# Turning three sample tiles apart instead of two doubled ones, in the RWKV-7 stage of a hybrid decoder step

## The chip, the cores and the metric

One Trainium2 chip, one NeuronCore. The metric is the device time of one execution in microseconds. A NeuronCore has TensorE (PE: its weight loads are shown apart, as PEld), VectorE (DVE), ScalarE (ACT), GpSimd (POOL), SyncE (SP), which issues DMAs, and 16 DMA engines. Each engine runs its own instructions in order and waits on semaphores for the others. TensorE's clock has two levels here, 1.2 and 2.4 GHz; the profile gives the granted clock as a share of the upper one, so 0.5 is the lower.

## The reference, cut to what matters

One inference step of a two-layer trunk in f32: D = 1024, 512 prompt tokens, and 8 sample sequences of 8 new tokens each. Layer 0 mixes with RWKV-7, layer 1 with a convolution module, and each is followed by an expert retrieval (PEER). The change is in the RWKV-7 mixer, which for each of 16 heads of size 64 keeps a 64x64 state S:

```
def step(S, inp):
    r_t, w_t, k_t, v_t, kk_t, a_t = inp
    sa = jnp.einsum('bhij,bhj->bhi', S, -kk_t)
    S = (S * w_t[:, :, None, :] + sa[..., None] * (kk_t * a_t)[:, :, None, :]
         + v_t[..., None] * k_t[:, :, None, :])
    return S, jnp.einsum('bhij,bhj->bhi', S, r_t)
```

The kernel does not step through the tokens. For a block of tokens it gathers the `sa` rows in a matrix U by solving a triangular system, and then gets the new state as a sum of two outer products over the block's tokens, U with b = kk*a, and V with k. The samples start from their own states (8 sequences), the prompt from zero.

## The kernel before, in words

Everything is feature major: 128 features in the partitions, 576 tokens (512 of the prompt, then 64 of the samples) along the free dimension. The stages follow one another: rmsnorm and low-rank inputs, then `wkv`, then the output projection, then one long stage for both retrievals and the convolution, which goes from about 1002 us to the end of the span. The change touches `wkv` alone. It runs from about 81 to 936 us.

`wkv` is a loop of 8 passes, written by hand for each engine, and a pass does one chunk of 128 features, that is two heads (e = 0, 1; 64 partitions each). The order on each engine is the order of the source; semaphores with named steps (class `Steps`) tie the engines. `X.value("name", i)` is the wait for step "name" of pass i. A pass of PE is:

1. small expansions and the three projections w, k, a, r, norm, v, g, bonus (each projection 32 matmul records of 288 columns),
2. turns of v, b, k into token-major tiles, the Gram matrices of four prompt blocks (L494), and six levels of a triangular inverse (L506, L513, L518),
3. the chain over the four prompt blocks: `rows_R` (L528, L531), `rows_U` (L538), `rows_Y_S` (L543 to L551), each of them waiting for a small copy of ACT or a state update of DVE; the samples' work lies between them,
4. the tail: `s_Y`, "mean" (L621, through `expand` in L449), `s_S` (L625), "var" (the `expand` of `ysq` behind it), after which the next pass begins with "w" (L449) and "k" (L443).

For the samples, three tiles of 128 features by 64 tokens have to be turned so that tokens stand in the partitions: b, k and v. Before, POOL copies the sample columns of all four factors at, rt, bt, kt side by side (`s_factors`, L846), and v's sample columns twice (`s_vv`, L849). PE turns two 128x128 tiles (L577, `s_tok`): b and k together, so that b's tokens are in partitions 0 to 63 and k's in 64 to 127, and v doubled, so that its tokens are in both halves. ACT copies the result into `stok` (L682). The sample state update `s_S` (L625) then takes b and k as one stationary operand over all 128 partitions, and `uv_exp` as moving operand: U expanded by sequence in partitions 0 to 63 (L817), V in 64 to 127 (L814). One matmul for each half of the sequences (h = 0, 1; 512 columns) sums both outer products. DVE takes the result at L825, and updates the state at L827 and L829.

In the trace an f32 matmul shows as two records with a weight load each, and a transpose as one.

Of the kernel before, what the change touches and what calls it, by code (L numbers as in the profile page):

```python
# [16 lines left out]
ALU = mybir.AluOpType  # L17
ACT = mybir.ActivationFunctionType
AX = mybir.AxisListType

P = 128
D = 1024
C = D // P
T = 512
SB, ST = 8, 8
NS = SB * ST
N = T + NS
# [8 lines left out]
LEVELS = 7  # L36
# [72 lines left out]
def unsq(view, axis, n):  # L109

    return view.unsqueeze(axis).to_broadcast(list(view.shape[:axis]) + [n] + list(view.shape[axis:]))
# [183 lines left out]
def wkv(nc, K, I, xm, y_out, hid_wa, hid_g, R, wo_loaded):  # L295
# [8 lines left out]
    f = lambda: R.cut(N)  # L304
# [3 lines left out]
    av, v_s, g_s, nrm = f(), f(), f(), f()  # L308
    e_pos, e_neg = f(), f()
    prev_at = R.at  # L310
    e_prev, factors, bon = f(), R.cut(4, N), f()
    at, rt, bt, kt = (factors[:, j, :] for j in range(4))
    s_factors, s_vv = R.cut(4, NS), R.cut(2, NS)

    ba, rk = lprev, sq
    y_s, yc, ysq, sd = e_pos, e_neg, e_prev, nrm
# [13 lines left out]
    co = [[Q0.cut(NB, P) for _ in range(2)] for _ in range(2)]  # L330
# [9 lines left out]
    Q = Region(K.arena, R.at)  # L340
    s_state = Q.cut(SB, P)
    Q2 = Region(K.arena, l_at)
    stok = Q2.cut(2, P)
    sL, sLT, sX, sXT, sG, sRB, sRK, sco, scoT = (Q2.cut(2, NS, parts=NS) for _ in range(9))
    sy1, sy2 = Q2.cut(2, NS, parts=NS), Q2.cut(2, NS, parts=NS)
    sr_tok, su_tok = Q2.cut(P, parts=NS), Q2.cut(P, parts=NS)
    assert Q2.at <= x_end
    Q3 = Region(K.arena, g_at)
    uv_exp = Q3.cut(SB, P)
    s_prod = Q3.cut(SB, P)  # L350

    wl = [K.sem(f"wkv_w{j}") for j in range(3)]
# [11 lines left out]
    act_s = Steps(K.sem("wkv_act"),  # L364
                  ["w", "k", "ksq", "a", "r", "norm", "exps", "v", "g", "tok_v", "tok_b", "tok_k", "gram_L0", "gram_L1"]
                  + [f"{x}{l}_{e}" for l in range(1, LEVELS) for x in ("y", "X") for e in range(2)]
                  + ["R0", "s_tok", "U0", "s_y1", "R1", "U1", "s_y2", "R2", "U2", "R3", "U3", "s_U"]
                  + ["Y", "ysq", "sd"], a_pass_ahead=True)
    dve_s = Steps(K.sem("wkv_dve"),
                  ["logs", "rk", "factors", "bonus"]  # L370
                  + [f"{x}{e}" for e in range(2) for x in ("maskLT", "level0_", "gramG", "gramRB", "gramRK")]
                  + [f"XT{l}_{e}" for l in range(1, LEVELS) for e in range(2)]
                  + ["s_gram", "state0", "s_X1", "state1", "s_X2", "state2", "s_RT", "state3"]
                  + ["s_y", "s_exp", "yc", "s_state", "y"], a_pass_ahead=True)
    pool_s = Steps(K.sem("wkv_pool"), ["s_copies"] + [f"co{l}_{e}" for l in range(1, LEVELS) for e in range(2)])
    assert NB == 4 and SLEVELS == 3
    ps = K.ps
    lev = lambda l, t: K.level[:, 2 * l + t, :]

    def later(view, l):  # L380

        return view.rearrange("p (g two r) -> p g two r", two=2, r=2 ** l)[:, :, 1, :]

    def packed(view, l):

        return view.rearrange("p (g r) -> p g r", r=2 ** l)

    with nc.Block() as block:
# [48 lines left out]
        def _(pe):  # L437
# [14 lines left out]
            with pe.Fori(0, C) as i:  # L452
# [19 lines left out]
                for src, bank, name, other, ready in ((v_s, 2, "tok_v", act_s, "v"), (bt, 0, "tok_b", dve_s, "factors"),  # L472
                                                      (kt, 1, "tok_k", act_s, "r")):
                    pe.wait_ge(other.sem, other.value(ready, i))
                    for b in range(NB):
                        last = pe.transpose(ps[:, bank, b * P:(b + 1) * P], src[:, b * P:(b + 1) * P], K.ident)
# [4 lines left out]
                for e in range(2):  # L481
                    q = slice(64 * e, 64 * e + 64)
                    for name, left, right, free in (("L", at, bt, ("g", "tok_k")), ("LT", bt, at, ("g", "tok_v")),
# [8 lines left out]
                        for b in range(NB):  # L492
                            t = slice(b * P, (b + 1) * P)
                            last = pe.matmul(ps[:, bank[e, name], t], left[q, t], right[q, t], start=True, stop=True)  # L494
# [3 lines left out]
                for l in range(1, LEVELS):  # L498
                    for e in range(2):
# [5 lines left out]
                        for b in range(NB):  # L505
                            last = pe.matmul(packed(ps[:, 4 * e, b * P // 2:(b + 1) * P // 2], l), co[l % 2][e][:, b, :],  # L506
                                             later(XT[:, e, b, :], l), start=True, stop=True)
                        last.then_inc(pe_s.at(f"y{l}_{e}"), 1)
                    for e in range(2):
                        if (l, e) == (1, 0):  # L510
                            pe.wait_ge(act_s.sem, act_s.value("gram_L1", i))
                        for b in range(NB):
                            last = pe.transpose(ps[:, 4 * e + 1, b * P:(b + 1) * P], XT[:, e, b, :], K.ident)  # L513
                        last.then_inc(pe_s.at(f"turn{l}_{e}"), 1)
                    for e in range(2):
                        pe.wait_ge(act_s.sem, act_s.value(f"X{l}_{e}", i))
                        for b in range(NB):
                            last = pe.matmul(ps[:, 4 * e + 2, b * P // 2:(b + 1) * P // 2], X[:, e, b, :], y1[e][:, b, :],  # L518
                                             start=True, stop=True)
# [4 lines left out]
                def rows_R(b):  # L524
                    t = slice(b * P, (b + 1) * P)
                    if b:
                        pe.wait_ge(dve_s.sem, dve_s.value(f"state{b - 1}", i))
                    pe.matmul(ps[:, 0, 0:P], at[:, t], sc_state[b % 2], start=True, stop=False)  # L528
                    for e in range(2):
                        q = slice(64 * e, 64 * e + 64)  # L530
                        last = pe.matmul(ps[:, 0, q], G[:, e, b, :], ptok[:, 2, b, q], start=False, stop=e == 1)  # L531
                    last.then_inc(pe_s.at(f"R{b}"), 1)
# [40 lines left out]

                pe.wait_ge(dve_s.sem, dve_s.value(f"XT{LEVELS - 1}_1", i))
                rows_R(0)
                for j, src in enumerate((s_factors[:, 2:4], s_vv)):
                    last = pe.transpose(ps[:, 4, j * P:(j + 1) * P], src.rearrange("p a b -> p (a b)"), K.ident)  # L577
                last.then_inc(pe_s.at("s_tok"), 1)
                for e in range(2):
                    q = slice(64 * e, 64 * e + 64)  # L580
                    for j, (left, right) in enumerate(((at, bt), (bt, at), (kt, at), (bt, rt), (kt, rt))):
                        last = pe.matmul(ps[0:NS, 5 + e, j * NS:(j + 1) * NS], left[q, T:N], right[q, T:N],
                                         start=True, stop=True)
# [10 lines left out]
                pe.wait_ge(state_loaded, i * 32 + 32)  # L594
                pe.wait_ge(dve_s.sem, dve_s.value("s_X2", i))
                for h in range(2):
                    pe.matmul(ps[:, 5 + h, :], s_factors[:, 0:2].rearrange("p a b -> p (a b)"), s_state[:, 4 * h:4 * h + 4, :], start=True, stop=True)
                for e in range(2):
                    q = slice(64 * e, 64 * e + 64)
                    last = pe.matmul(ps[0:NS, 4, q], sG[:, e, :], stok[0:NS, 1, q], start=True, stop=True)  # L600
                last.then_inc(pe_s.at("s_RT"), 1)
                rows_R(3)
                rows_U(3)
# [2 lines left out]
                for e in range(2):  # L606
                    q = slice(64 * e, 64 * e + 64)
                    last = pe.matmul(ps[0:NS, 7, q], sXT[:, e, :], sr_tok[:, q], start=True, stop=True)
# [5 lines left out]
                for e in range(2):  # L614
                    q = slice(64 * e, 64 * e + 64)
                    pe.matmul(ps[q, 4, 0:NS], su_tok[:, q], sRB[:, e, :], start=False, stop=False)
                    last = pe.matmul(ps[q, 4, 0:NS], stok[0:NS, 1, q], sRK[:, e, :], start=False, stop=True)
                last.then_inc(pe_s.at("s_Y"), 1)
                pe.wait_ge(dve_s.sem, dve_s.value("s_y", i))
                pe.wait_ge(act_s.sem, act_s.value("Y", i))  # L620
# [1 line left out]
                pe.wait_ge(dve_s.sem, dve_s.value("s_exp", i))  # L622
                for h in range(2):
                    hb = slice(4 * h, 4 * h + 4)
                    last = pe.matmul(ps[:, 6 + h, :], stok[:, 0, :], uv_exp[:, hb, :], start=True, stop=True)  # L625
                last.then_inc(pe_s.at("s_S"), 1)
                pe.wait_ge(act_s.sem, act_s.value("ysq", i))
                expand(K.headones, ysq, 0, "var")
# [2 lines left out]
        def _(act):  # L631
            act_s.begin(act)
            with act.Fori(0, C) as i:
# [45 lines left out]

                rows_R(0)  # L680
                act.wait_ge(pe_s.sem, pe_s.value("s_tok", i))
                act.activation(stok, ps[:, 4, 0:2 * P].rearrange("p (j f) -> p j f", f=P), ACT.Copy).then_inc(act_s.at("s_tok"), 1)  # L682
                rows_U(0)
                for b in (1, 2):
                    act.wait_ge(pe_s.sem, pe_s.value(f"s_y{b}", i))
                    last = act.activation(sy1, ps[0:NS, 7, 0:2 * NS].rearrange("p (e f) -> p e f", f=NS), ACT.Copy)
                    if b < SLEVELS - 1:
                        last = act.activation(sy2, ps[0:NS, 7, 2 * NS:4 * NS].rearrange("p (e f) -> p e f", f=NS), ACT.Copy)
# [15 lines left out]
        def _(dve):  # L704
            dve_s.begin(dve)
            tt, ts, stt = dve.tensor_tensor, dve.tensor_scalar, dve.scalar_tensor_tensor
            dve.memset(s_state, 0.0).then_inc(zeroed, 1)
            with dve.Fori(0, C) as i:
# [102 lines left out]
                dve.drain()  # L811
                tt(sr_tok, s_rows[0:NS, :], ps[0:NS, 4, 0:P], ALU.add).then_inc(dve_s.at("s_RT"), 1)
                update_state(3)
                tt(uv_exp[NS:P], unsq(stok[NS:P, 1, :], 1, SB), unsq(K.seq_of[NS:P], 2, P), ALU.mult)  # L814
                dve.wait_ge(pe_s.sem, pe_s.value("s_Y", i))
                dve.tensor_copy(y_s[:, T:N], ps[:, 4, 0:NS]).then_inc(dve_s.at("s_y"), 1)
                tt(uv_exp[0:NS], unsq(su_tok, 1, SB), unsq(K.seq_of[0:NS], 2, P), ALU.mult).then_inc(dve_s.at("s_exp"), 1)  # L817

                dve.wait_ge(pe_s.sem, pe_s.value("mean", i))
                stt(out=halves(yc), in0=of_banks(ps, 0), scalar=-1.0 / HD, in1=halves(y_s),  # L820
# [2 lines left out]
                for h in range(2):  # L823
                    hb = slice(4 * h, 4 * h + 4)
# [16 lines left out]
        @block.gpsimd  # L841
        def _(pool):
            with pool.Fori(0, C) as i:
                pool.wait_ge(dve_s.sem, dve_s.value("factors", i))
                pool.nop(nofuse=True)
                pool.tensor_copy(s_factors, factors[:, :, T:N])  # L846
                pool.wait_ge(act_s.sem, act_s.value("v", i))
                pool.nop(nofuse=True)
                pool.tensor_copy(s_vv, unsq(v_s[:, T:N], 1, 2)).then_inc(pool_s.at("s_copies"), 1)  # L849
                for l in range(1, LEVELS):  # L850
                    for e in range(2):
                        if l == 1:
                            pool.wait_ge(act_s.sem, act_s.value(f"gram_L{e}", i))
                        if l > 2:
                            pool.wait_ge(pe_s.sem, pe_s.value(f"y{l - 2}_{e}", i))
                        pool.tensor_tensor(co[l % 2][e], L[:, e], unsq(lev(l, 0), 1, NB), ALU.mult).then_inc(pool_s.at(f"co{l}_{e}"), 1)  # L856
# [989 lines left out]
```

## Time and profile before

| | |
|---|---|
| median of 3 runs | 4191.81 us (4189.78 to 4196.97) |
| the profiled execution | 4196.97 us, span 4195.2 us |
| mean granted TensorE clock | 0.939 |
| PE busy, of the span | 3525.0 us (84%), 12440 matmul records |
| DVE busy | 2866.3 us (68%) |
| ACT busy | 1480.4 us (35%) |
| POOL busy | 1482.4 us (35%) |
| in the stretch 81 to 927 us: PE, DVE, ACT, POOL busy | 775.5, 398.0, 255.1, 127.8 us; clock 0.92 |

A profile line names the source line (L625), the engine, the operation, the tensors as out<-in, the shape, and the count. "Idle before" is what the engine waited, with the instruction that ended the wait. Lines of the waits view read: who waited, for whom, total us, times, longest. In a timeline a row may be several instructions of one line merged: start, length, engine, line, shape, count. A stationary shape such as 64*128 is 64 partitions contracted by 128 columns; the moving shape follows. Matmul ends are modelled, so their starts are the better guide.

### The profile page before, as it was taken

What the parts mean: (1) busy time and instruction counts of PE and PEld (TensorE: products, weight loads), DVE (VectorE), ACT (ScalarE), POOL (GpSimd) and SP (SyncE); (2) the same over time, 40 slices, a digit from 0 to 9 for tenths busy, and PEclk for the clock granted to TensorE, in tenths of its full rate; (3) what the DMA queues carried; (4) which work ended last, traced back from release to release, by engine and by line L of the source; (5) the groups of instructions that cost most, each with busy time, mean ns of one, the idle gap of its engine ahead of it and who ended that gap; (6) DMA issues with size and microseconds to landing.
All of it is one profiled execution on the core that took longest, in us unless ns stands there. A gap on an engine that the chain in (4) does not pass through costs nothing.

```text
span 4195.2 us, 42635 instructions
## 1 busy us (share of the span) xinstructions
PE 3525.0 (84%) x12440; PEld 1962.3 (47%) x12440; DVE 2866.3 (68%) x6575; ACT 1480.4 (35%) x4136; POOL 1482.4 (35%) x1272
## 2 busy tenths in 40 slices
PE   5999999987888888898887977988799887777776
PEld 3777777766443333344443533444345333333332
DVE  5444444443766666789997777899977677777775
ACT  1233333321433333443344433423244333333333
POOL 0111111111444444444443454333334444444442
PEclk8899999999999999999998999998899999999999
DMA  2000000002999999999999999998989999999996
GB/s 76 22 22 22 22 22 22 17 13 99 427 427 426 427 427 427 426 423 394 406 413 405 394 427 425 424 337 321 331 342 376 427 425 426 427 427 427 427 427 293
DMA packets 228382, 1305.21 MB, mean 311 GB/s; under 512 B 58608, under 2 KB 61808, under 8 KB 80496
## 3 DMA queue, kind: packets, MB, share of 16 engines
q0 software_dynamic: 165888, 1208.03, 69.5%
q1 hardware_dynamic: 62320, 95.24, 6.5%
q8 instruction: 62, 1.02, 0.1%
q14 instruction: 112, 0.92, 0.1%
HBM read 1297.32 MB, written 5.86 MB: 311 GB/s over the span
## 4 chain that ended last, share of the span: by engine, by line
DMA 27%; DVE 21%; PE 19%; ACT 3%; issue 2%; DVEq 2%; POOL 1%; ACTq 0%; POOLq 0%
DMA arena<-in_uv,arena 27%; PE psum L1136 13%; DVE arena L1532 10%; DVE arena L1609 5%; PE psum L1100 4%; PE psum L1224 2%; POOL arena L1080 1%; DVE arena L1587 1%; ACT wbuf L1333 1%; DVE arena L1460 1%; DVEq L1611 1%; PE psum L1147 0%; DVE arena L1457 0%; ACT arena L1328 0%; DVE arena L1590 0%
## 5 line engine op out<-in xcount | busy, mean ns | idle before, releaser
L1136 PE MATMUL psum<-arena,wbuf 128*128 128x512 f32 (+1 forms) x4608 | 2120.8, 638 | 512.8 <-ACT wbuf L1333 511.3
L1080 POOL DMA_INDIRECT arena<-in_uv,arena x1152 | 1354.1, 1175 | 1792.0 <-PE psum L1136 1680.7
L1532 DVE SCALAR_TENSOR_TENSOR arena<-arena 128x1024 f32<-128x1024 f32 x1152 | 1396.8, 1223 | 544.2 <-DMA arena<-in_uv,arena 524.5
L1136 PEld LDWEIGHTS psum<-arena,wbuf 128*128 128x128 f32 (+1 forms) x4608 | 810.8, 193 | 1638.0 <-ACT wbuf L1333 825.9
L1324 ACT ACTIVATE arena<-arena 128x2 f32<-128x2 f32 x576 | 117.0, 203 | 1735.1 <-DVE arena L1532 1734.4
L1333 ACT ACTIVATE wbuf<-cst,arena 128x128 f32<-128x128 f32 (+1 forms) x1152 | 392.9, 388 | 41.4 <-issue 1.4
L1100 PE MATMUL psum<-arena,wbuf 128*128 128x256 f32 (+1 forms) x1024 | 287.8, 427 | 8.5 <-DVE arena L1543 5.8
L1328 ACT ACTIVATE arena<-arena 128x1 f32<-128x1 f32 x1152 | 276.7, 287 | 40.4 <-issue 0.7
L1100 PEld LDWEIGHTS psum<-arena,wbuf 128*128 128x128 f32 x1024 | 202.1, 200 | 129.1 <-issue 88.8
L1609 DVE SCALAR_TENSOR_TENSOR arena<-arena,par 128x256 f32<-128x256 f32 x480 | 232.0, 483 | 22.3 <-issue 1.0
L846 POOL COPY arena<-arena 128x256 f32<-128x256 f32 x8 | 3.2, 396 | 655.5 <-DVE arena L744 655.5
L443 PE MATMUL psum<-arena,wbuf 128*128 128x288 f32 x768 | 193.6, 411 | 0.3 <-DMA wbuf<-in_w_rkv 0.3
L767 DVE TENSOR_TENSOR arena<-arena,psum 128x256 f32<-128x256 f32 x96 | 40.6, 423 | 193.0 <-PE psum L518 193.0
L443 PEld LDWEIGHTS psum<-arena,wbuf 128*128 128x128 f32 x768 | 145.7, 191 | 46.1 <-ACT arena L638 3.1
L856 POOL TENSOR_TENSOR arena<-arena,level 128x512 f32<-128x512 f32 x96 | 122.7, 1304 | 97.5 <-PE psum L506 57.1
L1324 ACT ACT_TABLE_LOAD x104 | 133.4, 1283 | 28.3 <-DVE arena L1532 26.7
L1191 PE MATMUL psum<-arena 128*128 128x256 f32 (+1 forms) x512 | 136.8, 410 | 0.8 <-DMA arena<-in_w_pw 0.8
L1191 PEld LDWEIGHTS psum<-arena 128*128 128x128 f32 x512 | 98.0, 193 | 47.9 <-issue 25.2
L518 PE MATMUL psum<-arena 128*128 128x64 f32 x768 | 95.9, 278 | 12.1 <-ACT arena L669 12.1
L1312 ACT ACT_TABLE_LOAD x79 | 101.4, 1283 | 4.4 <-issue 0.3
L518 PEld LDWEIGHTS psum<-arena 128*128 128x128 f32 x768 | 89.3, 191 | 23.5 <-ACT arena L669 23.5
L1532 DVE DVE_READ_ACCUMULATOR arena<-arena 128x1 f32 x1152 | 94.9, 82 | 0.0
(252 smaller groups left out, 3327.4 us busy)
## 6 DMA issues: line engine op xcount, KB each, us to landing
wbuf<-in_w_q SPq DMA_DIRECT2D x64, 576.0 KB, 8.9
arena<-in_w_pw SPq DMA_DIRECT2D x48, 512.0 KB, 9.7
arena<-in_uv,arena POOLq DMA_INDIRECT x1152, 21.6
wbuf<-in_w_rkv SPq DMA_DIRECT2D x24, 512.0 KB, 3.5
wbuf<-in_w_o SPq DMA_DIRECT2D x8, 512.0 KB, 3.6
x<-in_x SPq DMA_DIRECT2D x1, 2304.0 KB, 8.1
arena<-in_state SPq DMA_DIRECT2D x16, 128.0 KB, 2.9
out_o_wkv_s<-arena SPq DMA_DIRECT2D x16, 128.0 KB, 2.6
```

The source lines that it names most:

```text
L443: last = pe.matmul(ps[:, bank + h, 0:HALF], w[:, k, :], src[:, k, h * HALF:(h + 1) * HALF], start=k == 0, stop=k == C - 1)
L518: last = pe.matmul(ps[:, 4 * e + 2, b * P // 2:(b + 1) * P // 2], X[:, e, b, :], y1[e][:, b, :], start=True, stop=True)
L856: pool.tensor_tensor(co[l % 2][e], L[:, e], unsq(lev(l, 0), 1, NB), ALU.mult).then_inc(pool_s.at(f"co{l}_{e}"), 1)
L1080: pool.indirect_dma_start(ring[:, g % RING, :], None, I["uv"][p // 2], bass.IndirectOffsetOnAxis(ap=idx[:, s % 4, j:j + 1], axis=0)).then_ ...
L1100: last = pe.matmul(ps[:, 7, 0:WIDTH[half]], K.w9[j][:, k, :], h[half][:, k, :], start=k == 0, stop=k == C - 1)
L1136: last = pe.matmul(out, diag[:, g % DIAGS, 0:P if u < NB else NS], ring[:, g % RING, D + e * 512:D + (e + 1) * 512], start=head == 0 and j ...
L1191: last = pe.matmul(out, wb[j][:, k, :], h[half][:, k, :], start=k == 0, stop=k == C - 1)
L1324: act.activation(gelu[:, q], dots[:, q], ACT.Gelu)
L1328: act.activation(coef[:, c:c + 1], gelu[:, c:c + 1], ACT.Copy, scale=share[:, s % 4, j + k:j + k + 1])
L1333: act.activation(diag[:, (g + k) % DIAGS, 0:P if u < NB else NS], same, ACT.Copy, scale=coef[:, c:c + 1]).then_inc(diag_ready, 1)
L1532: stt(out=row, in0=row, scalar=1.0, in1=tok[p % 2][:, UNITS[p % 2].index(u), :], op0=ALU.mult, op1=ALU.mult, accum_out=dots[:, g % RING:g ...
L1609: last = stt(out=out, in0=up[:, k:k + 2 * P], scalar=weight, in1=out, op0=ALU.mult, op1=ALU.add)
```

## The change

Of the four factors, POOL copies only at and rt, side by side (`s_at_rt`), since they still serve as one stationary operand at L597. The copy of v is gone, and so is POOL's wait for it. PE turns b, k and v in three transposes, each straight from its sample columns (128 features by 64 tokens), and the results all have their tokens in partitions 0 to 63. `stok` has three parts in place of two, over 64 partitions. The expanded U and V are two tiles of 64 partitions (`u_exp`, `v_exp`) in place of one of 128. The sample state update adds its two outer products in two matmuls per half, accumulated in PSUM: four of 64 partitions contracted in place of two of 128.

```
-    s_factors, s_vv = R.cut(4, NS), R.cut(2, NS)
+    s_at_rt = R.cut(2, NS)
...
-    stok = Q2.cut(2, P)
+    stok = Q2.cut(3, P, parts=NS)
...
-    uv_exp = Q3.cut(SB, P)
+    u_exp, v_exp = Q3.cut(SB, P, parts=NS), Q3.cut(SB, P, parts=NS)
...
-                for j, src in enumerate((s_factors[:, 2:4], s_vv)):
-                    last = pe.transpose(ps[:, 4, j * P:(j + 1) * P], src.rearrange("p a b -> p (a b)"), K.ident)
+                for j, src in enumerate((bt, kt, v_s)):
+                    last = pe.transpose(ps[0:NS, 4, j * P:(j + 1) * P], src[:, T:N], K.ident)
...
-                    pe.matmul(ps[:, 5 + h, :], s_factors[:, 0:2].rearrange("p a b -> p (a b)"), s_state[:, 4 * h:4 * h + 4, :], start=True, stop=True)
+                    pe.matmul(ps[:, 5 + h, :], s_at_rt.rearrange("p a b -> p (a b)"), s_state[:, 4 * h:4 * h + 4, :], start=True, stop=True)
...
-                    last = pe.matmul(ps[:, 6 + h, :], stok[:, 0, :], uv_exp[:, hb, :], start=True, stop=True)
+                    pe.matmul(ps[:, 6 + h, :], stok[:, 0, :], u_exp[:, hb, :], start=True, stop=False)
+                    last = pe.matmul(ps[:, 6 + h, :], stok[:, 1, :], v_exp[:, hb, :], start=False, stop=True)
...
-                act.activation(stok, ps[:, 4, 0:2 * P].rearrange("p (j f) -> p j f", f=P), ACT.Copy).then_inc(act_s.at("s_tok"), 1)
+                act.activation(stok, ps[0:NS, 4, 0:3 * P].rearrange("p (j f) -> p j f", f=P), ACT.Copy).then_inc(act_s.at("s_tok"), 1)
...
-                tt(uv_exp[NS:P], unsq(stok[NS:P, 1, :], 1, SB), unsq(K.seq_of[NS:P], 2, P), ALU.mult)
+                tt(v_exp, unsq(stok[:, 2, :], 1, SB), unsq(K.seq_of[0:NS], 2, P), ALU.mult)
...
-                tt(uv_exp[0:NS], unsq(su_tok, 1, SB), unsq(K.seq_of[0:NS], 2, P), ALU.mult).then_inc(dve_s.at("s_exp"), 1)
+                tt(u_exp, unsq(su_tok, 1, SB), unsq(K.seq_of[0:NS], 2, P), ALU.mult).then_inc(dve_s.at("s_exp"), 1)
...
-                pool.tensor_copy(s_factors, factors[:, :, T:N])
-                pool.wait_ge(act_s.sem, act_s.value("v", i))
-                pool.nop(nofuse=True)
-                pool.tensor_copy(s_vv, unsq(v_s[:, T:N], 1, 2)).then_inc(pool_s.at("s_copies"), 1)
+                pool.tensor_copy(s_at_rt, factors[:, 0:2, T:N]).then_inc(pool_s.at("s_at_rt"), 1)
```

(The two uses of V's token-major tile, at L600 and L617, read part 2 of `stok` in place of part 1.)

On PE, between the chain's first step `rows_R(0)` and the samples' Gram matrices (L582), counts are matmuls and shapes those of the result:

```order
 L528 MATMUL psum<-arena 128x128
 L531 MATMUL psum<-arena 128x64 x2
-L577 MATMUL psum<-cst,arena 128x128 x2
+L577 MATMUL psum<-cst,arena 64x128 x3
 L582 MATMUL psum<-arena 64x64 x10
 L535 REGISTER_ALU
```

Two turns with results of 128 partitions have become three with results of 64; nothing around them has moved.

On PE, in the tail of a pass, between "mean" (the first L449) and "var" (the second):

```order
 L449 MATMUL psum<-arena,cst 128x288 x2
 L622 REGISTER_ALU
-L625 MATMUL psum<-arena 128x512 x2
-L627 REGISTER_ALU
+L625 MATMUL psum<-arena 128x512
+L626 MATMUL psum<-arena 128x512
+L625 MATMUL psum<-arena 128x512
+L626 MATMUL psum<-arena 128x512
+L628 REGISTER_ALU
 L449 MATMUL psum<-arena,cst 128x288 x2
 L452 REGISTER_ALU
```

Two matmuls of 512 columns have become four, in the same place of the queue.

## Rows read from the trace of the kernel before

**Rows 1.** Waits, 81 to 927 us: waiter <- releaser, us in total, times, longest.
```profile
DVE arena L731 <- ACT arena L646: 53.3, 8, 8.5
DVE arena L825 <- PE psum L625: 15.4, 8, 2.7
```

**Rows 2.** Timeline, 184 to 206 us, the end of pass 0: start, length, engine, line.
```profile
190.84 1.22 DVE L817 TENSOR_TENSOR arena<-arena,cst 64x1024 f32<-64x1024 f32 x1
190.94 2.28 PE L449 MATMUL psum<-arena,cst 128*128 128x288 f32 x4 [1.19 <-DVE arena L816]
...
193.02 2.27 PE L625 MATMUL psum<-arena 128*128 128x512 f32 x4
...
194.06 0.68 ACT L699 ACTIVATE arena<-arena 128x576 f32<-128x576 f32 x1 [6.06 <-DVE arena L820]
...
195.13 1.13 PE L449 MATMUL psum<-arena,cst 128*128 128x288 f32 x4
...
196.19 1.23 PE L449 MATMUL psum<-arena 64*128 64x288 f32 x4
...
197.35 8.03 PE L443 MATMUL psum<-arena,wbuf 128*128 128x288 f32 x32
...
197.99 1.23 DVE L829 TENSOR_TENSOR arena<-arena 128x1024 f32<-128x1024 f32 x1
```

**Rows 3.** Windows from s_S to "var", passes 0 and 2, sum of all 8.
```profile
core 0: us, PE busy (x) PEld busy (x) DVE busy (x) ACT busy (x) POOL busy (x), PEclk, DMA share, GB/s
193.02:195.13 2.11, 2.11 (x6) 0.91 (x5) 0.76 (x1) 1.06 (x2) 0.00 (x0) 0.82 0.00 0
...
401.76:405.18 3.42, 3.42 (x6) 1.35 (x4) 0.76 (x1) 1.97 (x2) 0.00 (x0) 0.50 0.00 0
...
sum 21.78, PE 21.78 PEld 9.15 DVE 6.06 ACT 12.54 POOL 0.00; mean PE 2.72 PEld 1.14 DVE 0.76 ACT 1.57 POOL 0.00
```

**Rows 4.** Window from "var" to "k", pass 2, same columns.
```profile
405.18:407.53 2.35, 2.35 (x10) 1.36 (x8) 2.03 (x3) 1.04 (x2) 0.00 (x0) 0.95 0.00 0
```

**Rows 5.** Chain of waits, near 2335 us: start, length, what.
```profile
2335.44 3.43 PE psum L1136 x8
```

**Rows 6.** Timeline, 204 to 245 us, expansions "a", "g" and "bonus" of pass 1.
```profile
205.31 1.23 PE L449 MATMUL psum<-arena 64*128 64x288 f32 x4
...
223.07 1.13 PE L449 MATMUL psum<-arena 128*128 128x288 f32 x4
...
224.04 1.13 PE L449 MATMUL psum<-arena,cst 128*128 128x288 f32 x4
```

**Rows 7.** Timeline, 150 to 166 us, turning the sample tiles in pass 0.
```profile
156.62 0.63 PE L577 MATMUL psum<-cst,arena 128*128 128x128 f32 x2
...
157.18 2.03 PE L582 MATMUL psum<-arena 64*64 64x64 f32 x20
157.29 0.39 ACT L682 ACTIVATE arena<-psum 128x256 f32<-128x256 f32 x1
...
159.14 1.12 PE L538 MATMUL psum<-arena 128*128 128x64 f32 x4
```

**Rows 8.** Window of 1 us behind the turns in pass 0, columns as in rows 3.
```profile
157.00:158.00 1.00, 1.00 (x11) 0.82 (x11) 0.00 (x0) 0.53 (x2) 0.00 (x0) 0.50 0.00 0
```

**Rows 9.** Timeline of PE, 879 to 926 us, sample turns and "mean", pass 7.
```profile
894.20 0.39 PE L577 MATMUL psum<-cst,arena 128*128 128x128 f32 x2
...
919.64 2.28 PE L449 MATMUL psum<-arena,cst 128*128 128x288 f32 x4 [1.19 <-DVE arena L816]
```

**Rows 10.** Timeline, 204 to 245 us, Gram matrices on PE and POOL's copy of v.
```profile
227.34 0.29 POOL L849 COPY arena<-arena 128x128 f32<-128x128 f32 x1
...
227.95 8.66 PEld L494 LDWEIGHTS psum<-arena 64*128 64x128 f32 x80 [0.17 <-issue]
227.95 8.86 PE L494 MATMUL psum<-arena 64*128 64x128 f32 x80
...
229.82 1.26 POOL L856 TENSOR_TENSOR arena<-arena,level 128x512 f32<-128x512 f32 x1 [2.19 <-ACT arena L661]
```

More of the change, by code:

```diff
@@ L374, in wkv @@
                   + ["s_y", "s_exp", "yc", "s_state", "y"], a_pass_ahead=True)
-    pool_s = Steps(K.sem("wkv_pool"), ["s_copies"] + [f"co{l}_{e}" for l in range(1, LEVELS) for e in range(2)])
+    pool_s = Steps(K.sem("wkv_pool"), ["s_at_rt"] + [f"co{l}_{e}" for l in range(1, LEVELS) for e in range(2)])
     assert NB == 4 and SLEVELS == 3
@@ L596, in _ @@
                 for h in range(2):
-                    pe.matmul(ps[:, 5 + h, :], s_factors[:, 0:2].rearrange("p a b -> p (a b)"), s_state[:, 4 * h:4 * h + 4, :], start=True, stop=True)
+                    pe.matmul(ps[:, 5 + h, :], s_at_rt.rearrange("p a b -> p (a b)"), s_state[:, 4 * h:4 * h + 4, :], start=True, stop=True)
                 for e in range(2):
                     q = slice(64 * e, 64 * e + 64)
-                    last = pe.matmul(ps[0:NS, 4, q], sG[:, e, :], stok[0:NS, 1, q], start=True, stop=True)
+                    last = pe.matmul(ps[0:NS, 4, q], sG[:, e, :], stok[:, 2, q], start=True, stop=True)
                 last.then_inc(pe_s.at("s_RT"), 1)
@@ L616, in _ @@
                     pe.matmul(ps[q, 4, 0:NS], su_tok[:, q], sRB[:, e, :], start=False, stop=False)
-                    last = pe.matmul(ps[q, 4, 0:NS], stok[0:NS, 1, q], sRK[:, e, :], start=False, stop=True)
+                    last = pe.matmul(ps[q, 4, 0:NS], stok[:, 2, q], sRK[:, e, :], start=False, stop=True)
                 last.then_inc(pe_s.at("s_Y"), 1)
```

## The prediction

> **What bounds the kernel now.** I first asked where the changed instructions run: only between 81 and 936 us, in the eight passes of `wkv`. The long stage behind it has other limits (transfers, L1136, L1532), does the same work in the same order, and starts when `wkv` and the projection behind it have ended. So a microsecond added to `wkv` is a microsecond at the end, unless something in a pass covers it. The next view was the list of waits of that stretch. DVE waits for PE at L825, 15.4 us in 8 times [rows 1]: it stands ready for the sample state product and PE is late. The timeline of a pass's end shows the same from PE's side [rows 2]: "mean" starts at 190.94, `s_S` (L625) at 193.02, "var" at 195.13, "w" at 196.19, "k" at 197.35, each start following the last with nothing waited for after "mean". What "var" needs (ACT L699, ysq) ended at 194.06 + 0.68 = 194.74, so only 0.39 us before it was used; what `s_S` needs (DVE L817) ended at 192.06, 0.96 us early. From "mean" to the next pass's projections PE is thus the queue that sets the pace, and `s_S` stands in it.
>
> Is what follows also late when PE is late? DVE ends its part of the state at 197.99 + 1.23 = 199.22 [rows 2]; the expansion "a", which waits for that state, starts only at 205.31 [rows 6], 6.1 us later. And DVE then stands idle until the norm of the next pass (L731 waits for ACT L646, and so for PE's projections) for 53.3 us in 8 times, 6.7 us each [rows 1]. A tail that is 2 us later on DVE is absorbed there, and a PE that is 2 us later is not. In the last pass there are no next projections: DVE's chain L825 to the output is then the end, it starts with the same `s_S`, and is late by the same.
>
> **s_S, the main term.** Before: 2 matmuls of 512 columns, 4 records. After: 4 matmuls, 8 records of the same 512 columns; halving the contracted partitions does not halve the columns. At full clock, 8 records of 512 columns take 3.43 us [rows 5], 0.429 each. In this place the four old ones took 2.11 us in pass 0, 3.42 in pass 2, and 21.78 us over the eight passes, 2.72 each, at a granted clock of 0.82 in pass 0 and 0.50 in pass 2 [rows 3]. That is a clock that is low after the sparse chain and rises during `s_S`; in pass 2 it had not risen when `s_S` ended, but "var" and "w" behind it were at 0.95 [rows 4]. What is added stands behind the old four, where the clock is up. So I price the added four at the upper level: 4 x 0.429 = 1.72 us. The other end, all at the lower level, is 3.43 us.
>
> **What the smaller shape costs beside its columns.** PE goes from 128 contracted partitions ("mean") to 64 (`s_S`) and back ("var"). The nearest rows are expansions of 288 columns: "g" to "bonus", both of 128 partitions, 224.04 - 223.07 = 0.97 us [rows 6]; "var" (128) to "w" (64) 1.06; "w" (64) to "k" (128) 1.16 [rows 2]. So going in costs 0.09 and coming out 0.19: 0.28 us a pass. Its ends are nothing and, if the change stalls at each of the four matmuls, 4 x 0.28 = 1.1 us. The Trainium skill (TensorEngine Tiling (Array Packing), Key Properties) says that changing the tiling mode drains the engine; by that rule alone the cost is real but has no size, and the trace agrees with 0.09 and 0.19 us.
>
> **The turns (s_tok).** Two transposes of 128x128 become three with results of 64 partitions. Two records and the step to the Gram matrices took 157.18 - 156.62 = 0.56 us in pass 0 [rows 7]. A third record is 128 columns, a quarter of 0.429, 0.11 us at full clock; a second change of shape is 0.09, as above. I take 0.20. If each of the three turned into two records, as a product has, it would be 0.11 x 4 + 0.09 = 0.5; if the narrower tiles gained what the third costs, nothing. PE is also what sets the pace here: U0 (L538) follows the Gram matrices at once, at 159.14. ACT's copy grows from 128x256 to 64x384; it took 0.39 us from 157.29, and ACT's next piece is the copy of U0, which PE only begins at 159.14 [rows 7]. So 1.4 us cover what 128 elements more can cost, at most half of the 0.39 us for 256.
>
> **POOL, and what is nothing.** POOL loses the copy of v (0.29 us) and half of the other. Both ended at 227.63, and POOL then waited for ACT L661 until 229.82, 2.19 us [rows 10]. So nothing waited for the copies, and nothing is gained. The same rows bound a gain on DVE or PE from less traffic of POOL: it runs there for 0.6 us beside them, while PE has the Gram matrices before it. I take 0, with 0.1 us a pass as the gain's end. DVE's two expansions keep their 64x1024 shape (L817 1.22 us); only the partitions of V's change. SP's queue issues the same; the state's store follows L829 by a wait and moves with it, and its reload is wanted first at L597, some 70 us later. The tiles behind in SBUF move by 1 KB and lose nothing.
>
> **The sum.** 1.72 + 0.28 + 0.20 = 2.20 us a pass, 8 passes: 17.6 us. The profiled execution took 4196.97 us, so like for like 4214.6. That execution is the slowest of three, 5.2 us above their median. One reason is in the trace: from the sample turns to "mean" pass 0 needed 190.94 - 156.62 = 34.3 us, and pass 7 919.64 - 894.20 = 25.4 [rows 2, 7, 9], with the same instructions; in pass 0 the clock was at 0.50 already behind the turns [rows 8]. I take such a fall for something that comes and goes between executions, and set the sum on the median: 4191.81 + 17.6 = 4209.4 us, +0.42%.
>
> **The rivals.** (1) The forecast, 4209. Its own range is from 4191.8 + 8 x 1.5 = 4204 to 4191.8 + 8 x 2.8 = 4214, and some 4 us of clock luck on both sides.
> (2) Loads are laid bare. In `s_S` all weights and operands stand in the same 64 partitions. The Trainium skill (TensorE: Matmul & The Clock Gate, Part 3) says that a weight load overlaps a running matmul only where the row group differs; each load would then stand open. From rows: the loads of 64*128 take 8.66 us for 80 merged, beside 80 records that take 8.86 [rows 10], that is 0.11 us per record and load together, so within a run in the same 64 partitions they are hidden, and the rule doesn't hold for this chip's f32 pairs. If it did hold in `s_S`, where u and v alternate, a load of at most the 0.19 us that coming out of the shape costs would be added for each of 8: 8 x 8 x 0.19 = 12.2 us more, 4221.6.
> (3) The narrower product does not lift the clock. Now the rise comes in the course of a product over all 128 partitions, or just behind it. If half the partitions don't count, all 8 records run at the lower level: 6.86 us in place of 2.72, +4.14, with 0.48 for shapes and turns, and perhaps 1 us on "var": 8 x 5.6 = 45 us, 4237. Against it: the Gram matrices (64 partitions) ran 8.9 us at 0.11 us per 128 columns [rows 10], a quarter of the 0.43 for 512 [rows 5], so at full clock to their end. But that it holds is not that it rises, and "mean", which precedes, has 128.
> (4) Not slower: the clock gives it back. The place is the chain between the turns and "mean". It took 25.4 us in pass 7 and 34.3 in pass 0 for the same work, by where the clock falls and rises. All later passes come 2.2 us later each, so they meet those falls elsewhere. If the chain of an average pass became 1.1 us shorter, 8.8 us are back, and the result is within 0.2%; from 2.2 us a pass it is faster. For it speaks the size of the spread, against it that nothing in the change makes the chain denser, so it can as well turn out longer. Price of half the gain: 4200.
> (5) The added matmuls are covered. If PE had idled between `s_S` and "k", the added records would fill it and only the turns remain, 4191.8 + 1.6 = 4193. Against it stands the row of starts: no idle is shown before "var", "w" or "k", and the one known slack is 0.39 us.
>
> **How the numbers follow.** (1) 0.72, (2) 0.08, (3) 0.06, (4) 0.09, (5) 0.05. The range for 8 in 10 goes from 4199, which takes in half of (4), to 4222, which takes in (2); (3) and (5) are left out. A measurement of this kernel tells about 0.2% (8.4 us) from no change; the threshold is 4200.2. Slower: (1) but for a few hundredths, (2), (3) and a little of (4): 0.88. Same: 0.09. Faster, by (4) or (5) with luck: 0.03.
>
> **What would show it.** In the profile after: 64 records of 512 columns on the two lines of `s_S` in place of 32, and the time from the start of `s_S` to "var" about 2.72 + 1.72 + 0.1, some 4.5 us (4.0 to 5.3), with the second half of it at clock 1.0; starts "var" to "w" unchanged at 1.06; DVE's wait at L825 up by about 1.8 us to 3.7 a pass; DVE's idle before L731 still several us. The turns should be 3 records in 24, with the step to L582 up by 0.1 to 0.3. POOL has less work and a longer idle. I am wrong if `s_S` takes over 6.5 us at clock 0.5 (3), if each record of it is spaced by 0.6 us at full clock (2), if the time from the turns to "mean" differs by more than 1 us on average of the passes (4), or if PE shows an idle before "var" that the added matmuls have filled (5).

## The result, and the profile after

The changed kernel takes 4298.35 us (4292.86 to 4300.43), the one before on the same chip 4190.8 (4188.49 to 4196.97): ratio 1.0254, 95% interval 1.0243 to 1.0267. It is 107 us slower, six times the 17.6 us that I had added up.

The profile page of the changed kernel (span 4299.2 us, profiled execution 4301.01 us) has the loss at once: 124 us more busy time on PE, at most 3 us more on any other engine, and a lower mean clock, 0.912 against 0.939. First PE's line, then the clock in 40 slices; slices 1 to 10 cover `wkv`.

```profile
PE 3649.0 (85%) x12480; PEld 2031.2 (47%) x12480; DVE 2865.1 (67%) x6575; ACT 1482.2 (34%) x4136; POOL 1485.3 (35%) x1264
...
PEclk8788888877999999999999999998989999998898
```

PE has 40 records more (32 of the update, 8 of the turns). The instructions went where the order said; the rest is the same work at a lower clock. The timeline of the end of pass 0 answers to [rows 2]:

```profile
192.00 2.28 PE L449 MATMUL psum<-arena,cst 128*128 128x288 f32 x4 [0.96 <-DVE arena L817]
194.21 2.07 PE L625 MATMUL psum<-arena 64*128 64x512 f32 x2
...
196.08 1.91 PE L626 MATMUL psum<-arena 64*128 64x512 f32 x2
197.78 1.91 PE L625 MATMUL psum<-arena 64*128 64x512 f32 x2
199.49 1.91 PE L626 MATMUL psum<-arena 64*128 64x512 f32 x2
201.33 2.29 PE L449 MATMUL psum<-arena,cst 128*128 128x288 f32 x4
...
203.55 2.29 PE L449 MATMUL psum<-arena 64*128 64x288 f32 x4
...
205.77 9.50 PE L443 MATMUL psum<-arena,wbuf 128*128 128x288 f32 x32
```

"mean" starts within 1.1 us of where it did. Then `s_S` takes 201.33 - 194.21 = 7.12 us in place of 2.11, "var" and "w" 2.22 each in place of 1.06 and 1.16, and the k projection 9.50 in place of 8.03. Two records of 512 columns are spaced by 1.71 us, twice what [rows 5] has for two. The windows of `s_S` in passes 0, 2 and 7 with the sum of all eight (against 21.78 us in [rows 3]), then two windows of the k projection, show the clock. The granted clock is the third figure from the end of a line (PEclk, then DMA share and GB/s):

```profile
194.21:201.33 7.12, 7.12 (x9) 2.50 (x8) 0.76 (x1) 1.97 (x2) 0.00 (x0) 0.50 0.00 0
...
433.20:440.32 7.12, 7.12 (x10) 2.49 (x9) 0.76 (x1) 1.97 (x2) 0.00 (x0) 0.50 0.00 0
...
1023.31:1030.43 7.12, 7.12 (x9) 2.50 (x9) 0.76 (x1) 1.97 (x2) 0.00 (x0) 0.50 0.00 0
sum 56.97, PE 56.97 PEld 20.00 DVE 6.06 ACT 15.72 POOL 0.00; mean PE 7.12 PEld 2.50 DVE 0.76 ACT 1.97 POOL 0.00
```
```profile
207.00:208.00 1.00, 1.00 (x4) 0.71 (x3) 1.00 (x1) 0.00 (x0) 0.00 (x0) 0.50 0.89 170
208.00:209.00 1.00, 1.00 (x4) 0.71 (x3) 0.99 (x1) 0.00 (x0) 0.00 (x0) 0.61 0.29 54
```

The clock is at 0.50 through all of `s_S`, in every pass, and rises only at about 208.8 us, in the k projection. Before it rose during `s_S` or just behind it. A third part lies in the chain, from the turns to "mean". These are windows of passes 1 and 7 and the sum of all eight, first of the kernel before, then of the changed one:

```profile
267.68:296.38 28.70, 23.43 (x160) 17.09 (x160) 12.36 (x40) 4.12 (x14) 0.00 (x0) 0.76 0.00 1
...
894.20:919.64 25.44, 20.08 (x160) 15.11 (x160) 12.36 (x40) 4.13 (x14) 0.00 (x0) 0.89 0.00 0
sum 221.45, PE 179.97 PEld 135.10 DVE 98.97 ACT 33.06 POOL 0.00; mean PE 22.50 PEld 16.89 DVE 12.37 ACT 4.13 POOL 0.00
```
```profile
278.03:310.65 32.62, 28.54 (x160) 22.05 (x161) 12.28 (x40) 4.29 (x14) 0.00 (x0) 0.60 0.00 0
...
990.33:1021.09 30.76, 26.06 (x161) 19.30 (x161) 12.19 (x40) 4.28 (x14) 0.00 (x0) 0.67 0.00 0
sum 260.73, PE 226.83 PEld 172.93 DVE 98.12 ACT 34.27 POOL 0.00; mean PE 28.35 PEld 21.62 DVE 12.27 ACT 4.28 POOL 0.00
```

The same instructions but for one transpose take 39.3 us more, at a mean clock of 0.60 and 0.67 where it was 0.76 and 0.89. From the starts of the rows in each pass, the difference of the two spans, 104.0 us, divides so:

| stretch of a pass | before, sum | after, sum | more |
|---|---|---|---|
| turns to "mean" (the chain), 8 passes | 221.45 | 260.73 | 39.3 |
| "mean" to `s_S`, 8 | 16.6 | 17.7 | 1.1 |
| `s_S` to "var", 8 | 21.78 | 56.97 | 35.2 |
| "var" to "k", 7 | 15.9 | 31.0 | 15.1 |
| "k" to the Gram matrices, 7 | 214.2 | 226.8 | 12.6 |
| Gram matrices to turns, 7 | 278.1 | 279.6 | 1.4 |
| up to the first turns; behind the last "var" | | | 1.0; -1.7 |

The waits from 81 to 1040 us say the same of DVE: it waits 50.9 us at L826 for PE (before 15.4 at L825, [rows 1]).

```profile
DVE arena L732 <- ACT arena L647: 67.7, 8, 8.5
DVE arena L826 <- PE psum L626: 50.9, 8, 6.4
```

### The profile page after: what moved, and what is told of

Read it like the earlier page. It is cut to its first block, busy times and chain, and to the rows that moved or that the text cites. A ratio compares the mean times of both kernels' runs of the same rounds, so it can differ in the third digit from the quotient of the medians.

```text
span 4299.2 us, 42691 instructions
## 1 busy us (share of the span) xinstructions
PE 3649.0 (85%) x12480; PEld 2031.2 (47%) x12480; DVE 2865.1 (67%) x6575; ACT 1482.2 (34%) x4136; POOL 1485.3 (35%) x1264
## 3 DMA queue, kind: packets, MB, share of 16 engines
q0 software_dynamic: 165888, 1208.03, 67.7%
## 4 chain that ended last, share of the span: by engine, by line
DMA 26%; DVE 21%; PE 19%; issue 2%; ACT 2%; DVEq 2%; POOL 1%; ACTq 0%; POOLq 0%
DMA arena<-in_uv,arena 26%; PE psum L1134 12%; DVE arena L1530 10%; DVE arena L1607 4%; PE psum L1098 4%; PE psum L1222 2%; POOL arena L1078 1%; DVE arena L1585 1%; DVE arena L1458 1%; ACT wbuf L1331 1%; PE psum L1145 1%; DVE arena L1455 1%; DVEq L1609 1%; DVE arena L1462 0%; DVE arena L1588 0%
## 5 line engine op out<-in xcount | busy, mean ns | idle before, releaser
L1098 PEld LDWEIGHTS psum<-arena,wbuf 128*128 128x128 f32 x1024 | 205.6, 204 | 133.1 <-issue 93.5
L443 PE MATMUL psum<-arena,wbuf 128*128 128x288 f32 x768 | 206.3, 430 | 0.2 <-DMA wbuf<-in_w_rkv 0.2
L443 PEld LDWEIGHTS psum<-arena,wbuf 128*128 128x128 f32 x768 | 154.0, 203 | 53.2 <-issue 5.3
```

The costliest lines, as they stand in the source:

```text
L443: last = pe.matmul(ps[:, bank + h, 0:HALF], w[:, k, :], src[:, k, h * HALF:(h + 1) * HALF], start=k == 0, stop=k == C - 1)
L1098: last = pe.matmul(ps[:, 7, 0:WIDTH[half]], K.w9[j][:, k, :], h[half][:, k, :], start=k == 0, stop=k == C - 1)
```

## Experiments

Two theories of the tail were open. **S**: a product over 64 partitions does not lift the clock. **U**: the narrow turns pull it down, since in six of the eight passes the fall came within 1.1 us of their start. And for the chain **P**: what is lost there is only a matter of where in the pass the clock's fall lands, against **L**, that it grows with the length added. (In e7 and e4 a memset on DVE adds some 0.3 us a pass.)

**e1: narrow turns alone.** On the kernel before:

```
-                for j, src in enumerate((s_factors[:, 2:4], s_vv)):
-                    last = pe.transpose(ps[:, 4, j * P:(j + 1) * P], src.rearrange("p a b -> p (a b)"), K.ident)
+                for j, src in enumerate((bt, v_s)):
+                    pe.transpose(ps[0:NS, 4, j * P:(j + 1) * P], src[:, T:N], K.ident)
+                for j, src in enumerate((kt, v_s)):
+                    last = pe.matmul(ps[NS:P, 4, j * P:(j + 1) * P], src[:, T:N], K.ident, start=True, stop=True)
```

> Before, with the sample tiles turned straight from their 64 columns (four narrow turns: two transposes to partitions 0-63, two products with the identity to 64-127) and POOL copying only at and rt; the state update s_S stays at 128 contracted partitions. Theory S (a product over 64 partitions does not lift the clock): s_S takes 2.1 to 3.4 us and the clock is up by 'var'; time 4191 + 8 x 0.5 = 4195 (4188 to 4203). Theory U (the narrow turns make the clock fall early, as they coincide with the fall in 6 passes of the changed kernel): the clock falls at the turns in most passes, the time from turns to 'mean' is 32 to 34 us in place of 26.7, 4230 to 4240.

Measured: 4189.0 us (4183.84 to 4193.98), ratio 0.9994 (0.9984 to 1.0004), no change. The chain takes 220.86 us in its eight passes (before 221.45). U falls. The trace of the changed kernel speaks against it by itself: in those six passes the clock fell 0.1 to 1.1 us before the first turn, not behind it. Pass 2 shows it, where the turns start at 396.71:

```profile
396.00:396.50 0.50, 0.50 (x5) 0.50 (x6) 0.00 (x0) 0.00 (x0) 0.00 (x0) 1.00 0.00 0
396.50:396.70 0.20, 0.20 (x3) 0.20 (x3) 0.00 (x0) 0.00 (x0) 0.00 (x0) 0.52 0.00 0
```

**e2: narrow update alone.** The changed kernel with its turns made wide again:

```
-                for j, src in enumerate((bt, kt, v_s)):
-                    last = pe.transpose(ps[0:NS, 4, j * P:(j + 1) * P], src[:, T:N], K.ident)
+                for j in range(3):
+                    last = pe.transpose(ps[:, 4, j * P:(j + 1) * P], s_bkvv[:, j:j + 2].rearrange("p a b -> p (a b)"), K.ident)
```

> The changed kernel with its three turns made wide again (128 columns each, from a tile b,k,v,v that POOL copies), so that only the state update is narrow (64 contracted partitions). Theory S: 'mean' to 'k' is 13.8 us at clock 0.5 as in the changed kernel, the clock rises only in the k projection, about 4298 if the early fall in the chain follows from where the rise comes. Theory U: the tail stays long, but the clock falls late in the chain as before, 40 us less: 4258.

Measured: 4302.8 us (4286.71 to 4306.03), ratio 1.0257 (1.0225 to 1.0288); `s_S` 56.98 us in eight passes, the chain 260.75. The whole loss comes with the update.

**e3: as many records, but wide.** On the kernel before:

```
                     last = pe.matmul(ps[:, 6 + h, :], stok[:, 0, :], uv_exp[:, hb, :], start=True, stop=True)
+                    last = pe.matmul(ps[:, 6 + h, :], stok[:, 0, :], uv_exp[:, hb, :], start=True, stop=True)
```

> Before, with each of the two s_S matmuls issued twice (the second overwrites with the same sum): the same 8 records of 512 columns as in the changed kernel, but over 128 partitions. Theory S: the clock rises in the first half of s_S, each pass is 1.72 us longer: 4191 + 14 = 4205 (4198 to 4212). Theory L (it is the added length, through the place where the clock's fall and rise land, that costs the 100 us): 4240 or more.

Measured: 4231.72 us (4216.38 to 4236.13), ratio 1.0084 (1.0055 to 1.0112). Its eight `s_S` took 34.96 us, between 3.81 and 5.30, and "var" to "k" was back at 2.23: S holds. But it is 27 us above S's 4205, and they are in the chain. Windows of the chain, passes 2 and 6 and the sum:

```profile
377.67:401.83 24.16, 18.80 (x160) 14.19 (x160) 12.36 (x40) 4.14 (x14) 0.00 (x0) 0.94 0.00 1
...
815.53:850.02 34.49, 30.17 (x160) 22.98 (x160) 12.45 (x40) 4.18 (x14) 0.00 (x0) 0.55 0.00 0
sum 250.33, PE 213.50 PEld 163.16 DVE 99.32 ACT 33.32 POOL 0.00; mean PE 26.69 PEld 20.39 DVE 12.41 ACT 4.16 POOL 0.00
```

The same chain takes 24.2 us in one pass and 34.5 in another of one execution.

**e4 and e7: zero rows.** The changed kernel, contracted over 128 (e4) or 96 (e7) partitions, those above 64 zero in the stationary tile (e7 with `0:96` in the place of the first `:` of both tiles). The moving tile's added rows are not cleared:

```
+                dve.memset(stok_all[NS:P, 0:2, :], 0.0)
...
-                    pe.matmul(ps[:, 6 + h, :], stok[:, 0, :], u_exp[:, hb, :], start=True, stop=False)
+                    pe.matmul(ps[:, 6 + h, :], stok_all[:, 0, :], u_all[:, hb, :], start=True, stop=False)
```

> The changed kernel with the state update's four matmuls contracted over 128 partitions, the upper 64 rows of the stationary tile zero (one memset of 64x256 on DVE a pass), same columns and results. Theory S, by the count of rows addressed: 4205 (4198 to 4215), the clock up by the middle of s_S. If what matters is the work done in the cells and rows of zeros don't count: as the changed kernel, 4298. Theory L: 4240 or more.

> As the zero-padded version (4236 us, clock up in the middle of s_S), but contracted over 96 partitions, the upper 32 rows zero. If the clock's rise goes by a number of rows between 64 and 96, or by whether more than half the array is addressed: as zero-padded, s_S about 4.3 us, 4225 to 4245. If it needs all four quarters: s_S 7.1 us at clock 0.5 and about 4298.

Measured: e4 4236.41 us (4233.88 to 4240.85), ratio 1.0105 (1.0083 to 1.0127); e7 4233.2 us (4227.79 to 4234.94), ratio 1.0091 (1.0059 to 1.0123). `s_S` took 34.78 us in eight passes in e4 and 41.45 in e7 (after: 56.97). The timeline of e7's pass 0 shows the rise between the fourth and the fifth record:

```profile
190.03 1.92 PE L627 MATMUL psum<-arena 96*128 96x512 f32 x2
191.73 1.88 PE L628 MATMUL psum<-arena 96*128 96x512 f32 x2
193.44 1.03 PE L627 MATMUL psum<-arena 96*128 96x512 f32 x2
194.31 1.02 PE L628 MATMUL psum<-arena 96*128 96x512 f32 x2
195.17 1.14 PE L451 MATMUL psum<-arena,cst 128*128 128x288 f32 x4
```

So the partitions addressed count, and not what their weights are worth: with rows of zero weights the clock rises, over 96 partitions too, over 64 not. Adding useless rows makes the changed kernel 62 us faster. That e4 came to S's `s_S` but missed S's time is the chain again: 254.40 us, only 6 less than in the changed kernel. In e7 it is 234.19.

**e5 and e6: the added length.** Each `s_S` matmul three times (e5), or the first of the two twice (e6), all wide, diffs as in e3.

> Before, with each s_S matmul issued three times (12 records over 128 partitions, 3.44 us more of full-clock work a pass; doubled it was 1.72 us a pass and 41 us in all, of which 14 were the records). Theory P (the added records cost their own time, 27.5 us in all; the rest of a loss is where the clock's fall lands in the chain, which does not grow with what is added): 4218 plus or minus 12, so possibly below the doubled version's 4232. Theory L (the loss grows with the added length): 4191 + 2 x 41 = 4273.

> Before, with the first of the two s_S matmuls issued twice (6 records in place of 4 over 128 partitions, 0.86 us more a pass). Theory P: 4191 + 7 = 4198, plus what the fall's new place costs, 0 to 60. Theory L: 4191 + 0.5 x 41 = 4211.

Measured: e5 4217.29 us (4213.98 to 4221.16), ratio 1.0059 (1.0044 to 1.0074); e6 4206.49 us, ratio 1.0007 (0.9983 to 1.0032), where the ten times fall into two groups, 4180.5 to 4181.4 and 4206.1 to 4209.4. e5 does 1.72 us a pass more than e3 and is 14 us faster; its chain took 217.26 us. One binary, e6, is 10 us faster than the kernel before in four executions (mean clock 0.942 to 0.945) and 16 to 19 us slower in six (0.933 to 0.936). Only a slower one has a trace, with 228.59 us in the chain and 28.91 in `s_S`, so where the faster ones gain is not shown. The kernel before does it too: beside these runs, three of its 24 took 4207.6 to 4208.5 us, the others 4186.0 to 4192.9. So L falls and P is left: the added records cost their own time (`s_S` in e5 takes 28.4 us more than before), and beside it the chain is dealt anew: 29 us more in e3, 4 us less in e5.

**e8 and e9: idle products in PE's waits.** On the kernel before, results used by nobody: in e8 eight products of 256 columns in the chain, in e9 four before `s_U` and two before "mean", where PE waited for DVE anyway:

```
+                    pe.matmul(ps[:, bank, P:P + 256], K.ident, K.cst[:, 0:256], start=True, stop=True)
```

> Before, with 8 idle products a pass (128 partitions, 256 columns, the results used by nobody) where PE waits in the chain over the prompt blocks: in rows_Y_S before the wait for U (four), after S (three), before the wait for R in the last block (one). Each is 0.43 us of PE at full clock, 3.4 us a pass, of which some 2 us fall into waits of 0.3 to 0.9 us. Theory P: the clock holds from the level loop to 'mean', turns to 'mean' falls from 27.7 us to 23 to 25, 20 to 35 us gained in all, 4160 to 4170. If the fillers don't hold the clock: they cost 0.86 us each at the lower level, 8 x 4 = 32 us lost, 4223.

> Before, with idle products (128 partitions, 256 columns, the result used by nobody) in the two longest waits of PE in the chain's end: four before s_U, where PE waits 1.95 us for DVE's reduction, and two before 'mean', where it waits 1.19 us for y. At full clock they are 1.72 and 0.86 us and fit into the waits. Theory P (the clock is what is lost, and wide work keeps it): the clock is at its upper level at 'mean' in most passes, 'mean' to s_S to 'var' goes from 2.08 + 2.72 to about 1.1 + 1.8 us, 15 to 30 us gained in all, 4160 to 4178. If they come too late to keep the clock, they run at the lower level and push s_U and 'mean' by 1.5 and 0.5 us: 4207.

Measured: e8 4205.11 us (4200.43 to 4208.46), ratio 1.0025 (1.001 to 1.004); e9 4189.67 us (4173.98 to 4195.14), ratio 0.9994 (0.9985 to 1.0003). Both expectations of a gain missed. e8 held the clock longer in the chain (212.85 us in place of 221.45); `s_S` still began at the lower level (23.02 us in its eight passes). The gain was lost in one place, from the Gram matrices to the turns of pass 7: 63.7 us against 39.7 in the others. The timeline and two windows of it:

```profile
845.58 15.84 PE L494 MATMUL psum<-arena 64*128 64x128 f32 x80
```
```profile
850.00:855.00 5.00, 5.00 (x28) 5.00 (x28) 2.08 (x3) 0.37 (x1) 0.00 (x0) 0.50 0.00 0
...
895.00:900.00 5.00, 5.00 (x26) 5.00 (x26) 0.42 (x1) 0.77 (x2) 0.00 (x0) 0.50 0.00 0
```

There the clock fell about 1 us into the Gram matrices (64 partitions), and neither they, 80 records in 15.8 us, nor the level loop lifted it for over 50 us. PE had waited 1.32 us before the turns of v, b and k that precede them, but it does so in passes with no fall as well (pass 6). In the seven other passes the same stretch ran at full clock, but for the last 0.4 us in pass 0. So narrow work can hold the clock, and does not always. e9 did what it was to do at "mean", but its chain was 224.32 us, with two passes of 32.6 and 32.8.

**e10: the changed kernel with the six idle products of e9.**

> The changed kernel with the same six idle products. Theory S in its first form (a product over 64 partitions does not lift the clock, but holds it, as the Gram matrices do): where the clock is up at 'mean' it stays up through s_S (3.5 us for 8 records) and the projections begin at full clock: 50 to 90 us gained, 4210 to 4250. If a product over 64 partitions of 512 columns does not even hold it, the clock falls in s_S or behind it: 4280 to 4300.

Measured: 4184.37 us (4177.04 to 4205.69), ratio to before 0.9988 (0.9976 to 0.9999), that is 114 us faster than the changed kernel and better than any theory had it. Timeline of pass 0 (L536 is the second pair of idle products), then windows of `s_S` in pass 0 and the sum, and of the chain in pass 3 and the sum:

```profile
187.68 1.13 PE L536 MATMUL psum<-cst 128*128 128x256 f32 x4
189.22 1.23 PE L449 MATMUL psum<-arena,cst 128*128 128x288 f32 x4 [0.41 <-DVE arena L823]
190.38 1.12 PE L631 MATMUL psum<-arena 64*128 64x512 f32 x2
191.34 1.02 PE L632 MATMUL psum<-arena 64*128 64x512 f32 x2
192.20 1.02 PE L631 MATMUL psum<-arena 64*128 64x512 f32 x2
193.06 1.02 PE L632 MATMUL psum<-arena 64*128 64x512 f32 x2
194.01 1.24 PE L449 MATMUL psum<-arena,cst 128*128 128x288 f32 x4
```
```profile
190.38:194.01 3.63, 3.63 (x10) 1.41 (x9) 0.76 (x1) 1.97 (x2) 0.00 (x0) 1.00 0.00 0
...
sum 29.02, PE 29.02 PEld 11.28 DVE 6.06 ACT 15.73 POOL 0.00; mean PE 3.63 PEld 1.41 DVE 0.76 ACT 1.97 POOL 0.00
```
```profile
474.06:498.06 24.00, 21.18 (x173) 15.90 (x173) 12.24 (x40) 4.28 (x14) 0.00 (x0) 1.00 0.00 0
...
sum 213.81, PE 193.31 PEld 144.81 DVE 98.02 ACT 34.26 POOL 0.00; mean PE 24.16 PEld 18.10 DVE 12.25 ACT 4.28 POOL 0.00
```

With the clock up at "mean", the narrow update keeps it up to its end: 3.63 us, all at 1.00. The same update in e9, wide and at 1.00 too, took 14.58 us in eight passes, 1.82 each. The difference, 1.81 us a pass, is what the change of the update costs by its instructions, and near what the prediction had for it.

**e11 and e12: both sets of idle products**, on the kernel before; in e12 the eight in the chain are 128 columns wide in place of 256.

> Before, with both sets of idle products: the eight in the chain (256 columns, e8) and the six in the two long waits at its end (e9). Theory P: turns to 'mean' 25.7 us or a little more in all passes but perhaps the first, in place of 27.7, 'mean' to 'var' 3.0 in place of 4.8: 8 x 3.8 = 30 us gained, 4155 to 4168. If they only move the fall into another place (the level loop before the turns), nothing is gained: 4190.

> As the version before it, with the eight products in the chain half as wide (128 columns, 0.21 us each at full clock). If they still hold the clock, turns to 'mean' is 24.3 to 25 us and some 8 us more are gained: 4148 to 4160. If they are too thin for it, falls are as in e9: 4180 to 4190.

Measured: e11 4170.74 us (4163.17 to 4193.54), ratio 0.9956 (0.9942 to 0.997); e12 4168.86 us (4161.36 to 4194.74), ratio 0.9964 (0.9945 to 0.9982). Both beat both kernels, the one before by 21 and 22 us by the medians and by 18 and 15 by the ratios, and both fell short of the gain expected. Windows of e12's chain, passes 0 and 1 and the sum:

```profile
156.88:190.52 33.64, 32.52 (x188) 26.09 (x188) 12.48 (x40) 4.18 (x14) 0.00 (x0) 0.66 0.00 1
266.07:290.78 24.71, 22.71 (x188) 17.62 (x188) 12.40 (x40) 4.13 (x14) 0.00 (x0) 1.00 0.00 1
...
sum 212.22, PE 197.17 PEld 154.23 DVE 99.45 ACT 33.22 POOL 0.00; mean PE 24.65 PEld 19.28 DVE 12.43 ACT 4.15 POOL 0.00
```

Five of eight passes run through at 1.00. The two versions can't be told apart by these times.

## Why the prediction was wrong, step by step

- **PE sets the pace from "mean" on, and DVE and ACT have cover: right.** DVE's idle before the norm (L732) did not shrink, 67.7 us in 8 times, though its tail came 5 us later.
- **s_S, 4 more records at 0.429 us, "what is added stands behind the old four, where the clock is up": this is the step that failed.** The count and the full-clock price were right (e10 less e9: 1.81 us with shape costs), and the reading of [rows 3] that the clock rises during `s_S` was too. But I took the rise for something that comes at its time, whatever runs. The old `s_S`, behind "mean", was what brought it about. Replacing it by a narrow one took that away: 7.12 us in place of the 4.5 that I expected, and "var", "w" and the first 3 us of "k" at half clock too. These three come to 35.2 + 15.1 + 12.6 = 62.9 us, of which 14.5 are the records.
- **Rival 3 was the right mechanism**, at a chance of 0.06 and a price of 45 us. I had argued against it with the Gram matrices while saying myself that to hold is not to rise. What decided was a row that I had not looked for: a stretch in which a 64-partition product alone has to lift the clock. There was none, so the chance should have been near that of the forecast. It was priced too low as well: I let the clock be up by "var", but behind a narrow product that has not lifted it nothing wide has run yet except "var" itself, then a narrow "w".
- **The chain, "some 4 us of clock luck on both sides": wrong by ten times.** The spread of 25.4 to 34.3 us between two passes stood in the rows, and I took the long one for an accident of one execution. It is none: pass 0 took 28.9 to 34.4 us in every trace here. Nor are the passes of a loop independent draws: in e7 the last four chains took 29.04 us each, in e1 they went to and fro between 24.8 and 29.3, so the same luck can strike in all. e3 against e5 shows what it is worth. The chain cost 39.3 us here, and the runs do not part what of this belongs to the narrow update and what to the new length of a pass: with the update over 128 partitions (e4) it was still 33.0 us above before, over 96 (e7) 12.7. Rival 4 had this mechanism, but priced only its favourable side.
- **Shape: 0.28 us a pass forecast, about 0.2 found.** In e10 the eight narrow records leave 3.63 - 8 x 0.429 = 0.20 us, in e9 the four wide ones 1.82 - 1.72 = 0.10; "var" to "k" is 2.33 in place of 2.23; "mean" to `s_S` is the same, 1.16 and 1.17. So there is some 0.1 us at either end of the narrow run. That is in line with the drain at a change of tiling mode that the Trainium skill names (TensorEngine Tiling (Array Packing), Key Properties); no run shows that it is this drain.
- **Rival 2, loads laid bare: right to reject.** In e10 u and v alternate in the same 64 partitions at 0.86 us for two records, the rate of [rows 5]. The rule of the Trainium skill (TensorE: Matmul & The Clock Gate, Part 3) on loads in one row group does not show in these f32 products.
- **The turns: 0.20 us forecast, 0.10 found.** At full clock, pass 5 after, from the turns to L582 it is 755.12 - 754.70 = 0.42 us; in e9, with wide turns, 264.42 - 264.10 = 0.32. Three records stayed three.

```profile
754.70 0.49 PE L577 MATMUL psum<-cst,arena 128*64 128x128 f32 x3
755.12 1.20 PE L582 MATMUL psum<-arena 64*64 64x64 f32 x20
```

- **POOL: nothing, right.** e1 drops its copies too, and is no faster.

What stays open: which feature of the level loop and the chain decides whether a fall comes at the turns or 7 to 22 us later. The runs show that the turns' shape does not decide it (e1) and that early falls come with a wide update too (e3), and that the falls land elsewhere when the pass has another length (e3, e5, e6). Nor is it shown why the clock fell at the Gram matrices in one pass of e8 alone.

## What to carry to other kernels

A product that stands where TensorE's clock rises can also be what makes it rise; before its shape is changed, ask what will lift the clock in its place, and look for a row in which the new shape has done it alone. Price a stretch that runs at either level of the clock by both, for all passes of a loop at once and not for one. Where PE waits on a serial chain, wide idle products in the waits can be worth more than what they cost: here they took back the whole loss (e10), and with more of them the kernel before became some 20 us faster (e11, e12).

## What the runs showed of the hardware

- 8 records of 512 columns over 64 partitions did not lift the clock from 1.2 GHz in 7.12 us without a gap, in any of 8 passes, behind a wide "mean" of 2.2 us; over 96 or 128 partitions as many records did, after 0.8 to 4.3 us of them at 0.5 (e3, e4, e7; from length and mean clock of their windows), with zero weights in the added rows as well (e4, e7).
- The same 8 narrow records, begun at 2.4 GHz, ran at it to their end (3.63 us, clock 1.00), and so did the narrow "w" behind them. But the Gram matrices, narrow too, once ran at 1.2 GHz from their second microsecond to their end, 15.8 us in place of 8.9 (e8), so holding isn't certain either.
- One kernel can have two times, 27 us (0.65%) apart, at mean clocks of about 0.944 and 0.935 (e6); two groups in the times of one kernel are a sign to look at the clock of each pass.
